# One ring of weight slabs through both layers, and the output banks emptied ahead of the retention steps in four slabs of a decoder trunk

## The reference, cut to what matters

```python
h = rms_norm(x, norm_g);  proj = h @ w_in          # q, k, v of both branches, g_r, gates
y_a = stick_breaking_attention(...) @ sb_w_out     # 8 heads
o_r = head_group_norm(retention(qr, kr, vr)) * silu(g_r)   # 4 heads, chunks of 128
y_b = o_r @ ret_w_out
x = x + (sigmoid(g_a) * y_a + sigmoid(g_b) * y_b) @ w_o
a, b = split(rms_norm(x, norm_g) @ w_up)
x = x + (silu(causal_conv(a) + conv_b) * b) @ w_down
```

## Time and profile before

| | |
|---|---|
| median of 3 runs | 1645.99 us (1645.76 to 1647.21) |
| profiled execution, its own time | 1645.74 us |
| its span, first to last instruction | 1643.7 us |
| PE busy | 1631.0 us |
| DVE busy | 938.0 us |
| ACT busy | 643.5 us |
| POOL busy | 174.1 us |
| mean granted TensorE clock | 0.998 |

### The profile page before, as it was taken

How to read it: one execution, slowest core, us unless ns; L and a number is a source line. 1 busy time by engine, 2 the same in 40 slices (tenths; PEclk the granted TensorE clock), 3 DMA queues, 4 the chain that set the end, 5 groups by cost and what they waited for, 6 DMA issues and landing times.

```text
span 1643.7 us, 19541 instructions
## 1 busy us (share of the span) xinstructions
PE 1631.0 (99%) x7432; PEld 1353.9 (82%) x7432; DVE 938.0 (57%) x1108; ACT 643.5 (39%) x756; POOL 174.1 (11%) x162
## 2 busy tenths in 40 slices
PE   9999999999999999999999999999999999999998
PEld 7888888888888888888888888888888888888887
DVE  7268865666665666533252797655656666656222
ACT  5244334423345445522143533334323554444212
POOL 4001221000310000002120012200004000000020
PEclk9999999999999999999999999999999999999999
DMA  5342222222323233232233322222232222323232
GB/s 190 99 120 77 77 77 90 73 69 91 101 90 102 91 100 96 95 102 91 83 122 97 109 78 77 77 90 77 66 101 99 94 94 97 101 90 102 90 103 77
DMA packets 44236, 154.44 MB, mean 94 GB/s; under 512 B 4928, under 2 KB 5056, under 8 KB 44176
## 3 DMA queue, kind: packets, MB, share of 16 engines
q1 hardware_dynamic: 42192, 148.92, 27.9%
q10 hardware_dynamic: 1872, 4.33, 1.0%
q0 software_dynamic: 112, 0.33, 0.1%
HBM read 149.36 MB, written 2.10 MB: 92 GB/s over the span
## 4 chain that ended last, share of the span: by engine, by line
PE 94%; DVE 3%; POOL 1%; issue 1%; ACT 1%; DMA 1%; SPq 0%; POOLq 0%; DVEq 0%; ACTq 0%
PE ps L854 29%; PE ps L856 29%; PE ps L855 29%; PE ps L944 1%; PE ps L933 1%; PE ps L968 1%; POOL beta L361 1%; PE ps L976 1%; PE ps L964 1%; DMA w_raw<-wts 1%; PE ps L918 0%; PE ps L922 0%; PE ps L1062 0%; DVE w_lo L573 0%; PE ps L955 0%
## 5 line engine op out<-in xcount | busy, mean ns | idle before, releaser
L854 PE MATMUL ps<-u_hi,w_hi 128*128 128x512 f32 x1344 | 528.6, 393 | 0.0
L856 PE MATMUL ps<-u_hi,w_lo 128*128 128x512 f32 x1344 | 523.4, 389 | 0.0
L855 PE MATMUL ps<-u_lo,w_hi 128*128 128x512 f32 x1344 | 523.1, 389 | 0.0
L573 DVE TENSOR_TENSOR w_lo<-w_raw,w_hi 128x1024 fp32r<-128x1024 f32 x275 | 352.3, 1290 | 290.2 <-ACT w_hi L381 286.4
L381 ACT ACTIVATE w_hi<-w_raw 128x1024 fp32r<-128x1024 f32 x275 | 288.1, 1056 | 289.1 <-DMA w_raw<-wts 282.8
L856 PEld LDWEIGHTS ps<-u_hi,w_lo 128*128 128x128 f32 x1344 | 252.3, 188 | 53.1
L854 PEld LDWEIGHTS ps<-u_hi,w_hi 128*128 128x128 f32 x1344 | 252.4, 188 | 51.6 <-issue 0.5
L855 PEld LDWEIGHTS ps<-u_lo,w_hi 128*128 128x128 f32 x1344 | 252.5, 188 | 51.3 <-issue 0.5
L856 PE MATMUL ps<-g_hi,w_lo 128*128 128x512 f32 x352 | 136.9, 389 | 0.0
L854 PE MATMUL ps<-g_hi,w_hi 128*128 128x512 f32 x352 | 136.9, 389 | 0.0
L855 PE MATMUL ps<-g_lo,w_hi 128*128 128x512 f32 x352 | 136.9, 389 | 0.0
(11 more groups left out here) (166 smaller groups left out, 1949.3 us busy)
## 6 DMA issues: line engine op xcount, KB each, us to landing
w_raw<-wts SPq DMA_DIRECT2D x275, 512.0 KB, 3.4
x<-xt SPq DMA_DIRECT2D x8, 256.0 KB, 7.3
q<-q ACTq DMA_DIRECT2D x8, 256.0 KB, 3.8
out<-rows SPq DMA_DIRECT2D x8, 256.0 KB, 2.9
dec<-decay ACTq DMA_DIRECT2D x2, 514.0 KB, 4.6
cs<-rope ACTq DMA_DIRECT2D x2, 512.0 KB, 3.6
w_raw<-wts SPq DMA_DIRECT2D x2, 256.0 KB, 4.4
cst<-consts POOLq DMA_DIRECT2D x1, 192.0 KB, 4.7
```

The source lines that it names most:

```text
L573: nc.vector.tensor_tensor(w_lo[:, s, :], w_raw[:, s, :], w_hi[:, s, :].bitcast(F32), ALU.subtract).then_inc(s_lo, 1)
L854: nc.tensor.matmul(dst, a_hi, b_hi, start=start, stop=False)
L855: nc.tensor.matmul(dst, a_hi, b_lo, start=False, stop=False)
L856: return nc.tensor.matmul(dst, a_lo, b_hi, start=False, stop=stop)
```

## The change

It has two parts.

The first is the ring. The slot of a slab becomes its number over both layers modulo four, on every engine, and SyncE's loops over the layers become one loop of 68 rounds of four loads, each of which waits for the slab four before it. The waits written out by hand, the tail of each layer's loop, and `SLOT_USES` go.

The second is VectorE's order. The block that reads a unit's banks becomes a function `unit_out(l, i)` with the same text. For the slabs 52 to 55 it is called ahead of the parts of the retention steps (`RT_AT`, `RA_AT`, `RB_AT`, `RC_AT`); for all others it stays where it was.

```diff
-SLOT_USES = [(SLABS - s + RING - 1) // RING for s in range(RING)]
...
-            def load(l, slot, i):
-                sp.dma_start(w_raw[:, slot, :], wts[bass.ds(l * SLABS + i, 1), :, :]
+            def load(slot, n):
+                sp.dma_start(w_raw[:, slot, :], wts[bass.ds(n, 1), :, :]
...
-            for l in range(DEPTH):
-                for i, need in enumerate((3, 4, 1, 2)):
-                    if l > 0:
-                        sp.wait_ge(s_free, l * SLABS + need)
-                        load(l, i, i)
-                with sp.Fori(1, SLABS // RING) as r:
-                    for j in range(RING):
-                        sp.wait_ge(s_free, l * SLABS + r * RING + j + 1)
-                        load(l, j, r * RING + j)
-                for i in range(SLABS // RING * RING, SLABS):
-                    sp.wait_ge(s_free, l * SLABS + i + 1)
-                    load(l, i % RING, i)
+            assert DEPTH * SLABS % RING == 0
+            with sp.Fori(1, DEPTH * SLABS // RING) as r:
+                for j in range(RING):
+                    sp.wait_ge(s_free, r * RING + j + 1)
+                    load(j, r * RING + j)
...
-                s = i % RING
-                act.wait_ge(s_land[s], l * (16 * SLOT_USES[s]) + g * 16 + 16 * (i // RING + 1))
+                s, use = (l * SLABS + i) % RING, (l * SLABS + i) // RING
+                act.wait_ge(s_land[s], g * 16 + 16 * (use + 1))
...
-                s = i % RING
+                s = (l * SLABS + i) % RING
...
+            def unit_out(l, i):
+
+                u = unit_at(i)
+                if u:
...
+                    if YA0 <= i < YB0:
+                        unit_out(l, i)
                     if i in TURN_AT:
...
-                    u = unit_at(i)
-                    if u:
...
+                    if i < YA0 or i >= YB0:
+                        unit_out(l, i)
                     split_lo(l, i + AHEAD)
...
-                    slot = i % RING
+                    slot = (l * SLABS + i) % RING
```

More of the change, by code:

```diff
@@ L297, in _ @@
             for i in range(1, RING):
-                load(0, i, i)
+                load(i, i)
                 load_x(2 * i)
                 load_x(2 * i + 1)
-            for l in range(DEPTH):
-                for i, need in enumerate((3, 4, 1, 2)):
-                    if l > 0:
-                        sp.wait_ge(s_free, l * SLABS + need)
-                        load(l, i, i)
-                with sp.Fori(1, SLABS // RING) as r:
-                    for j in range(RING):
-                        sp.wait_ge(s_free, l * SLABS + r * RING + j + 1)
-                        load(l, j, r * RING + j)
-                for i in range(SLABS // RING * RING, SLABS):
-                    sp.wait_ge(s_free, l * SLABS + i + 1)
-                    load(l, i % RING, i)
+            assert DEPTH * SLABS % RING == 0
[3 more added lines that the diff above has]
+                    load(j, r * RING + j)
             for n, (tt, h) in enumerate(PIECES):
@@ L595, in gained @@
                                         ALU.mult).then_inc(s_xgd, 1)
+            def unit_out(l, i):
+                u = unit_at(i)
+                if u:
+                    kind, j, n = u
+                    if i == UP0 - 1:
+                        dve.wait_ge(s_part, l * 4 + 1)
+                    else:
+                        slab_done(l, i)
+                    for t in range(2):
+                        src = ps[:, 2 * (n % 2) + t, :]
+                        k = 2 * j + t
+                        if kind == "qk":
+                            which, p = j % 2, 2 * (j // 2) + t
+                            dve.wait_ge(s_r, l * 3 + 2)
+                            if j > 0:
+                                dve.wait_ge(s_ql, l * 16 + 4 * (j - 1) + 2 * t + 2)
+                            nc.vector.scalar_tensor_tensor(out=qk_tmp[:, t, :], in0=src, scalar=(0.125, 1.0)[which],
+                                                           in1=rinv[:], op0=ALU.mult, op1=ALU.mult).then_inc(s_tile, 1)
+                        if kind == "rot":
+                            which, h = j // 2, 2 * (j % 2) + t
+                            step = l * 24 + 3 * k
+                            dve.wait_ge(s_csr, l * 2 + 2)
+                            if k >= 2:
+                                dve.wait_ge(s_rot, step - 3)
+                            nc.vector.tensor_tensor(qk_r[:, h, which, :], src, cs[:, 0, :], ALU.mult).then_inc(s_rot, 1)
+                            nc.vector.tensor_tensor(rtmp[0:64, t, :], ps[64:128, 2 * (n % 2) + t, :], cs[64:128, 1, :],
+                                                    ALU.mult).then_inc(s_rot, 1)
+                            nc.vector.tensor_tensor(rtmp[64:128, t, :], ps[0:64, 2 * (n % 2) + t, :], cs[0:64, 1, :],
+                                                    ALU.mult).then_inc(s_tile, 1)
+                            dve.wait_ge(s_rot, step + 2)
+                            dve.wait_ge(s_tile, l * TILES + TILE_CREDIT + 2 * n + t + 1)
+                            nc.vector.tensor_tensor(qk_r[:, h, which, :], qk_r[:, h, which, :], rtmp[:, t, :], ALU.add).then_inc(s_rot, 1)
+                        if kind in ("gr", "gate"):
+                            dst = sg if kind == "gr" else gate
+                            nc.vector.tensor_tensor(dst[:, k, :], src, rinv[:], ALU.mult).then_inc(s_tile, 1)
+                        if kind == "ya":
+                            dve.wait_ge(s_gate, l * 16 + k + 1)
+                            nc.vector.tensor_tensor(gate[:, k, :], gate[:, k, :], src, ALU.mult).then_inc(s_tile, 1)
+                        if kind == "yb":
+                            dve.wait_ge(s_gate, l * 16 + 8 + k + 1)
+                            nc.vector.tensor_tensor(gate[:, 8 + k, :], gate[:, 8 + k, :], src, ALU.mult).then_inc(s_tile, 1)
+                            dve.wait_ge(s_tile, l * TILES + TILE_CREDIT + 2 * n + t + 1)
+                            nc.vector.tensor_tensor(gate[:, k, :], gate[:, k, :], gate[:, 8 + k, :], ALU.add).then_inc(s_m, 1)
+                        if kind == "wo":
+                            if i == UP0 - 1 and t == 1:
+                                slab_done(l, i)
+                            nc.vector.tensor_tensor(x[:, k, :], x[:, k, :], src, ALU.add).then_inc(s_tile, 1)
+                    if kind == "qk":
+                        for t in range(2):
+                            p = 2 * (j // 2) + t
+                            for b in (0, 64):
+                                h = 2 * p + b // 64
+                                hi = (q2, k2)[j % 2][b:b + 64, h, :]
+                                lo = q_lo[p][b:b + 64, b // 64, :] if j % 2 == 0 else k2[64 - b:128 - b, h, :]
+                                if j % 2 == 0:
+                                    dve.wait_ge(s_qz, l * SB_PAIRS + p + 1)
+                                dve.wait_ge(s_qh, l * 16 + 4 * j + 2 * t + b // 64 + 1)
+                                nc.vector.tensor_tensor(lo, qk_tmp[b:b + 64, t, :], hi.bitcast(F32), ALU.subtract).then_inc(s_ql, 1)
+                    if kind == "yb":
+                        for t in range(2):
+                            k = 2 * j + t
+                            dve.wait_ge(s_mh, l * 8 + k + 1)
+                            nc.vector.tensor_tensor(m_lo[:, k, :], gate[:, k, :], m_hi[:, k, :].bitcast(F32),
+                                                    ALU.subtract).then_inc(s_ml, 1)
+                    if kind == "wo":
+                        for t in range(2):
+                            u_low(l * 16 + 8, 2 * j + t, pcol(l, PAR_FFN + 2 * j + t))
@@ L1088, in operand @@
                                 pe.wait_ge(s_ul, l * 16 + 8 + k + 1)
-                        unit_slab((UP0 + j) % RING, u_hi, u_lo, 4 * (j % 2), j % 2 == 0, j % 2 == 1, h, operand, bank_free)
+                        unit_slab((l * SLABS + UP0 + j) % RING, u_hi, u_lo, 4 * (j % 2), j % 2 == 0, j % 2 == 1, h, operand, bank_free)
                         if first and j == 0:
```

## The result

The changed kernel takes 1644.01 us (median of 21 runs, 1642.72 to 1645.56), the kernel before 1646.32 us beside it (21 runs, 1645.39 to 1647.46). The ratio is 0.9985, with a 95% interval from 0.9979 to 0.9991: 2.4 us less by the means, 2.3 us by the medians. The forecast was 2.36 us less. The interval (1.5 to 3.5 us) excludes no change, but a gain of 1.53 us and one of 3.26 us, the two alternatives of the prediction, would fit it too; the traces tell them apart.

The account below looks back on a forecast made before the run. TensorE, busy 1631.0 of 1643.7 us, was taken to run at its matmul pace with four short stalls within reach. 1.58 + 0.78 = 2.36 us less gave 1643.6 us, range 1642.2 to 1646.0.

Parts of the forecast that it names:

- the two alternatives of the prediction: Gain of 1.53 us if only shown idle time is saved (1644.5), or 3.26 us with slab 138 (1642.7).
- Slab 55: Last retention slab, held by VectorE's late multiplications into `gate`; new order removes 0.79 us per layer, 1.58 us in all.
- The other steps: VectorE's new order at 52, 54 and 55: zero; at 55 `sg` about 0.3 us later, hidden by slab work.
- Slab 139: Where the layers meet: the ring loads it about 11 us earlier, so its whole stall goes, 0.78 us.
- The working in which VectorE waits out GpSimd's sum: Shared port pair at slab 139: `w_lo` ends at 822.7, still 1.9 us ahead of need.
- Slab 138: Where the layers meet: late behind VectorE's additions to `x`, which the change leaves ahead; zero gain, upper bound 0.90 us.
- rival A: Slab 138 starts on time too: 3.26 us less, 1642.7 us; chance 0.07.
- B: GpSimd takes slab 139's gain back, needing 2 us further blocking; 1.58 us left, 1644.4 us; chance 0.06.
- C: Something else holds slabs 55 and 139 as before, so no effect: 1645.2 to 1646.0 us; chance 0.06.
- D: Last head's chain delays TensorE behind slab 55 if over 5.5 us later; slower, 1649.3 us or more; chance 0.04.
- What a measurement can tell: About 0.2% (3.3 us) was taken as the least difference a measurement tells from no change.

Follow-up runs that it names:

- The experiment with the moved split: Changed kernel with VectorE's split of slab 138 moved ahead of its last three additions to x in layer 1: 1642.49 us, again 1643.34 us.
- the two delays: Changed kernel with 8 or 18 added statistics on VectorE in step 53, ahead of the last head's statistics: 1643.74 and 1653.11 us.

## Why the prediction was right

**Slab 55 (1.58 us).** Right in mechanism and size: the stall went in both layers, worth 1.5 us by the rest. By the starts, `ret_cross` to transposes takes 12.21 us in place of 12.99 in the first layer and 12.20 in place of 12.97 in the second, 1.55 us in all. The second layer before:

```profile
1170.33 1.46 PE L976 MATMUL ps<-state,q_x 128*128 128x256 f32 x6
...
1183.30 1.03 PE L1062 MATMUL ps<-cst,ynorm 128*128 128x128 f32 x8
```

and after:

```profile
1169.52 1.46 PE L975 MATMUL ps<-state,q_x 128*128 128x256 f32 x6
...
1181.72 1.03 PE L1061 MATMUL ps<-cst,ynorm 128*128 128x128 f32 x8
```

The multiplications ran from 358.30 to 359.59, in front of the statistics. I had put the shift of the statistics relative to `ret_cross` at up to 0.2 us: it was 1.50 in place of 1.49 us, 0.01.

**The other steps (zero).** Right. At 55 `sg` came 1.40 us behind the first transpose where it had been 1.07, 0.33 us later, and nothing waited for it.

**Slab 139 (0.78 us).** Right, 0.8 us: from slab 137's last matmul to slab 140 it takes 829.95 - 817.97 = 11.98 us in place of 830.81 - 818.02 = 12.79. The order of VectorE's work was the one written down; `w_lo` took 2.31 us beside GpSimd, 0.12 us over the 2.19 that I had put as the worst, and ended at 822.54, 2.0 us ahead of need. The working in which VectorE waits out GpSimd's sum had it at 822.7; that wait is in the trace, and cost nothing, as forecast.

**Slab 138 (zero).** Right: the same 0.56 us of idle time. The experiment with the moved split confirms the reason, and that rival A's 0.90 us were to be had with one more edit (0.8 measured).

**The rivals.** B had the right neighbour, but needs 2 us more of blocking; 3.8 us of added work cost 0.9. C is refuted by both separate parts. D's place was right, but its threshold was not: the tightest need behind slab 55 is not the transposes (5.5 us) but slab 56's banks, emptied in step 54 behind the same chain. From the changed kernel's rows that slack is 4.6 us; the two delays put it between 3.77 and 8.37 us, and the row for `gate` at slab 56 shows the wait. The price was too low for that reason, and because it left out the clock: D's working has a chain that comes 8.3 us later cost 3.3 us over the kernel before, and with 8.37 us of added work the rest is 6.9 us over it (1293.3 and 1286.4). The smaller slack (0.9 us a layer) and the slower slab 56 (1.1 and 0.9 us) make 3.8 us, and the two figures differ by 3.6.

**What a measurement can tell.** The prediction put this at 0.2% (3.3 us). That was too coarse: with 21 runs of each kernel the interval is 0.06% to either side, about 1.0 us, and the change of 2.4 us is clear of noise.

## What to carry to other kernels

On an engine that is busy 99% of the span, price a stall by the starts of its instructions against the undisturbed pace, restart included; the idle time shown (1.53 us here) undercounts what its removal gives (2.4 us). When a load arrives late, look at what the next engine is doing when it would arrive early: the ring freed slab 139, but slab 138 only once the split was also moved ahead of work that waits for TensorE. And compare kernels that differ by a tenth of a per cent over a part of the trace that leaves the scattered head out.

## What was not expected of the hardware

The first matmuls run at either of two paces, 0.23 or about 0.43 us apart, in executions of the same kernel, the slower one for 2.7 to 5.7 us where it occurs. With it `ret_cross` starts 0.7 to 2.5 us later than in the earliest profile (358.10 to 359.84 against 357.38). The slow pace is that of the stretch above with a granted clock of 0.50, yet the clock column reads 1.00 in the head, so there the level is read from the starts alone. The Trainium skill, "TensorE: Matmul & The Clock Gate", section "What's actually happening", says that how many first matmuls run slowly differs from run to run; the trace agrees, with those numbers. Waits of 0.5 us left the granted clock at 1.00, and one of 2.58 us was followed by 3 us at 0.50.
